# A two-part transformer kernel on one core: a new order in the first stage, weight pieces loaded in halves, and retention's gating and gate row moved

## The chip, the cores and the metric

The kernel runs on one core of one Trainium2 chip as a single launch. The metric is the device time of that launch in microseconds; the time shown is the median of three runs. PE is TensorE, DVE is VectorE, ACT is ScalarE, POOL is GpSimd, SP is the engine that issues the weight loads.

## The reference, cut to what matters

The input is 256 tokens of width 1024 in float32. Two blocks run one after the other, each with two layers. The parts that the change touches are the first mixer of the first block (a gated delta rule over six heads, beside a windowed attention), and in the second block the two mixers (stick-breaking attention and retention).

```
def gated_delta_rule(q, k, v, g, beta):
    ...
    gam = jnp.cumsum(gc, axis=-1)
    decay = jnp.exp(jnp.where(incl, gam[..., :, None] - gam[..., None, :], -jnp.inf))
    kk = jnp.einsum('bhnid,bhnjd->bhnij', kc, kc)
    lower = jnp.eye(c) + jnp.where(strict, bc[..., :, None] * kk * decay, 0.0)
    sol = lax.linalg.triangular_solve(lower, rhs, left_side=True, lower=True, unit_diagonal=True)
...
def even_mixer(x, ...):
    q_a, k_a, v_a, z_a, b_a, a_a, q_b, k_b, v_b = jnp.split(x @ w_in, EVEN_SPLITS, axis=-1)
    qkv = silu(causal_depthwise_conv(concatenate([q_a, k_a, v_a]), conv_w))
    q_a, k_a = l2_normalize(q_a) * GDN_DK ** -0.5, l2_normalize(k_a)
    o_a = gated_delta_rule(q_a, k_a, v_a, g, beta)
    o_a = rms_norm(o_a, norm_w) * silu(z_a)
    o_b = dilated_attention(q_b, k_b, v_b, rel_bias)
    return concatenate([o_a, o_b]) @ w_out
...
def retention(h, positions, w_in, gn_g, w_out):
    q, k, v, g = jnp.split(h @ w_in, [D_MODEL, 2 * D_MODEL, 4 * D_MODEL], axis=-1)
    ...  # per head and chunk of 128: (q k^T * decay mask) v, plus the carried state
    o = ((o - mu) * rsqrt(var + LN_EPS)).reshape(B, S, 2 * D_MODEL) * gn_g
    return (silu(g) * o) @ w_out
...
def second_block(x, c, ...):
    for i in range(DEPTH):
        shift, scale, gate = adaln_params(c, ada_w[i, 0], ada_b[i, 0])
        y = stick_breaking_attention(h, ...) if i == 0 else retention(h, ...)
        x = layer_norm_2(ALPHA * x + (1.0 + gate) * y, ...)
        ...
        y = grouped_moe(h, ...)          # 16 experts
        x = layer_norm_2(ALPHA * x + (1.0 + gate) * y, ...)
```

## The kernel before, in words

Each engine has its own program, written out by hand in stages: `even`, `ffn(0)`, `odd`, `ffn(1)`, `sb_stage`, `moe(0)`, `ret`, `moe(1)`. Nothing is scheduled by a compiler; each engine runs its list in order and waits on counters of the others (`t`, `v`, `a`, `g` are the counters of PE, DVE, ACT and POOL; `t.did(name)` notes a count, `v.wait_ge(*t(name))` waits for it). Where several independent chains run at once, `weave(units, steps, width, fill)` makes the order: round by round one step of each live unit, and after each round one piece of other work, written `(None, k)`. All engines walk the same list.

**First stage, `even`.** Projections are tiles of 128 output channels by 256 tokens; `conv(n)` is one of 24 of them (8 matmuls on PE; for n under 18 a scaled copy on ACT and three fused multiply-adds on DVE; convs 18 to 23 are the gate z, only copied). `L2` weaves the normalization of six pairs of q and k tiles (ACT squares, PE sums over the partitions with a matrix of ones, ACT takes Ln and Exp, DVE multiplies) with convs 12 to 17. `GDN` weaves four units u (a half of the tokens by three heads) of 17 steps with convs 18 to 23 and 13 pieces `ada` of a later modulation, whose weights share the ring of slots. Step 0 of a unit: DVE copies two columns into 128x384 operands (`a`, `b`), PE makes `gdB` and `gdb` from them (three matmuls each), DVE adds the mask into `DT`, ACT takes four exponentials (`gdDT`), and DVE multiplies `LT = DT * gdb`. Step 1 makes `gkk` and `gqk`. After GDN an RMS norm runs over six head tiles of 256 columns, each: square (ACT), sums (PE), Ln, Exp (ACT), two multiplications (DVE). Then `down` multiplies all eight 128-row tiles of the result with `w_out` (pieces `woe`), 32 matmuls of 512 columns; tiles 6 and 7 come from the windowed attention.

**Narrow stages, `sb_stage` and `ret`.** Their weights (`ws`, `wso`, `wr`, `wrv`, `wro`, 2 MB a piece, 24 pieces) come in turn into two slots of the ring. A piece is loaded by SP in one transfer, when the last use of the piece that had the slot before is counted. Each piece is cut into four chunks: ACT rounds a chunk to `ringhi` (`high_half`, four buffers, so chunk i waits for PE to be done with chunk i-4), DVE writes the rest to `ringlo` (`low_half`), and PE multiplies the parts. In `ret`, PE makes 4 + 20 projection tiles (`pr`; the first 16 are q and k, rotated through PE and three DVE operations each; the last eight and then eight more in `GATES` are the gate g), row products of `wrv` (`vr`, 0 to 3, made mean-free on DVE by `centered`), then the gate row of the modulation (`gate_row(2, Q.gk)`: DVE spreads a column to 128x1024, PE turns it with 8 matmuls, DVE copies the result), and then `RETU`: eight heads u of three steps (0: scores `rs`, DVE multiplies by the decay mask into `rp`; 1: values `ro`, ACT squares and copies; 2: sums `rv`, ACT Ln and Exp, DVE scales), three at a time, with the ten pieces `GATES` after the rounds. For u under 4, step 2 on DVE also gates: scale, multiply by the gate, round to `ghi`, subtract to `glo`, for two tiles f = 2u, 2u+1. The other eight tiles are gated inside the last product `down_split` (16 chunks of `wro`, f = 0 to 15, 12 matmuls of 512 columns a chunk).

**MoE stages.** Their expert weights use all eight slots; SP issues each load when its slot is free, in the order of `all_loads`, and stands still at the first load that is not free yet.

Of the kernel before, what the change touches and what calls it, by code (L numbers as in the profile page):

```python
# [175 lines left out]
L2 = weave(6, 2, 3, 6)  # L176
GDN = weave(4, 17, 4, 6 + ADA)
# [7 lines left out]
RETU = weave(8, 3, 3, len(GATES))  # L185

# [21 lines left out]
def all_loads():  # L208
# [15 lines left out]
    out += two[:2] + [("wro", j) for j in range(3)] + two[2:4] + [("wro", 3)] + two[4:]  # L224
# [12 lines left out]
def all_slots():  # L237


    out, used, last, turn, seen, narrow = {}, {}, {}, 0, [0, 0], 0  # L240
    for name in LOADS:
        if name[0] in NARROW:
            i, turn = narrow % 2, 0
            narrow += 1
            last[2] = name
        elif name[0] in ("mg", "mu", "md"):
# [12 lines left out]
PLACE = all_slots()  # L259
def consts():  # L260
# [66 lines left out]
def emit(nc, ctx, ins, out):  # L327
# [57 lines left out]
    s_ring = [sem(f"ring{i}_landed") for i in range(WIDE)]  # L385
    s_row, s_dec = sem("rows_landed"), sem("decay_landed")
# [43 lines left out]
    def chunk(n, i):  # L430

        src, kind, c = CHUNKS[n][i]
        lo = PLACE[src][0] * 4096
        hi = ringhi[:, i % 4, :]
        k = 4 if kind == "D" else 8
        whole, low = (ap[:, lo:lo + 4096].rearrange("p (k n) -> p k n", k=k) for ap in (ring, ringlo))
        if kind == "T":
            at = (slice(None), slice(None), slice(c * 128, c * 128 + 128))
        else:
            at = (slice(None), slice(2 * c, 2 * c + 2) if kind == "R" else slice(c, c + 1), slice(None))  # L440
        return whole[at], hi.rearrange("p (k n) -> p k n", k={"T": 8, "R": 2, "D": 1}[kind]), low[at]
# [31 lines left out]
    with ExitStack() as st:  # L473
# [18 lines left out]
        E.tmp3 = [E.u[i][k] for i in range(2) for k in ("a", "DT", "LT")]  # L492
# [67 lines left out]
    with ExitStack() as st:  # L560
# [11 lines left out]
        Q.gk = m.ap[:, m.top:m.top + 1024]  # L572
# [37 lines left out]
    def tensor():  # L610
# [32 lines left out]
        def first_tiles(n, src, tag, xT=xT):  # L643


            view = slot(src, 8)

            def half(c, h):
                tk = slice(h * 128, h * 128 + 128)
                for k in range(8):  # L650
                    r = mm(banks[c][:, tk], view[:, k, c * 128:c * 128 + 128], xT[:, k, tk], k == 0, k == 7)
                return r

            turn_x(n, 0)
            t.wait_ge(*arrived(src))
# [81 lines left out]
        def down_split(n, tag, i0, high, low, ready):  # L737
# [5 lines left out]
            for f, h in order:  # L743
                _, hi, lo = chunk(n, i0 + f)
# [93 lines left out]
        def even():  # L838
# [76 lines left out]
            for n in range(6):  # L915
# [398 lines left out]
        def ret():  # L1314
# [7 lines left out]
            gate_row(2, Q.gk, v)  # L1322
            i = 28
            for u, k in RETU:
# [24 lines left out]
                else:  # L1349
# [5 lines left out]
                       lambda f: v("gsplit", f))  # L1355
# [14 lines left out]
    def vector():  # L1370
# [119 lines left out]
        def even():  # L1490
# [63 lines left out]
            v.wait_ge(*a("l2", 5))  # L1554
            for u, k in GDN:
                if u is None:
                    ada_piece(0, k - 6)
# [3 lines left out]
            for n in range(6):  # L1561
                v.wait_ge(*a("rms", n))
                o = E.oT[:, n, :]
                tt(o, o, E.tmp3[n][:, 0:256], ALU.mult).then_inc(s_dve, v.did())
                stt(o, o, C("gnw"), E.QT[:, 18 + n, :], ALU.mult, ALU.mult).then_inc(s_dve, v.did("rms", n))
# [45 lines left out]

        def gdn(u, k):
# [7 lines left out]
            if k == 0:  # L1620
                copy(v3(m["a"]), col3(36, n0)).then_inc(s_dve, v.did())
                copy(v3(m["b"]), col3(24, n0)).then_inc(s_dve, v.did("gd_ab", u))
                tt(v3(m["DT"]), v3(src("gdB", u)), k3("cmt"), ALU.add).then_inc(s_dve, v.did("gdDT", u))
                v.wait_ge(*a("gdDT", u))
                tt(m["LT"], m["DT"], src("gdb", u), ALU.mult).then_inc(s_dve, v.did("free", "gdb", u))
# [435 lines left out]
        def ret():  # L2061
# [52 lines left out]
            gate_row(2, Q.gk)  # L2114

            def gated(u, d, o):
                g_ = Q.gT[:, 2 * u + d, :]
                stt(g_, o, C("rgn", 2 * u + d, 2 * u + d + 1), g_, ALU.mult, ALU.mult).then_inc(s_dve, v.did("rout", u))
                v.note("gated", 2 * u + d)

            def gated_low(u, d):
                f = 2 * u + d
# [5 lines left out]
            for u, k in RETU:  # L2128
                if u is None:
# [4 lines left out]
                    if kind == "vr":  # L2134
                        centered(j)
                    continue
# [9 lines left out]
                elif k == 2:  # L2146
                    v.wait_ge(*a("rv", u))
                    for d in range(2):
                        od = o[:, d * 256:d * 256 + 256]
                        if u < 4:  # L2150
                            tt(od, od, w[:, 0:256], ALU.mult).then_inc(s_dve, v.did())
                            v.wait_ge(*a("gT", 2 * u + d))
                            gated(u, d, od)
                            copy(Q.ghi[:, u + 8 * d, :], Q.gT[:, 2 * u + d, :]).then_inc(s_dve, v.did())
                            gated_low(u, d)
                        else:
                            tt(Q.qk[:, u + 8 * d, :], od, w[:, 0:256], ALU.mult).then_inc(s_dve, v.did("unit", u))
            for f in range(16):
                low_half(6, i + f + 3)
                if f < 8:  # L2160
                    u, d = 4 + f // 2, f % 2
                    v.wait_ge(*a("gT", 8 if u < 6 else 12))
                    gated(u, d, Q.qk[:, u + 8 * d, :])
                if 0 < f < 9:
                    v.wait_ge(*a("ghi", 7 + f))
                    gated_low(4 + (f - 1) // 2, (f - 1) % 2)
# [14 lines left out]
    def scalar():  # L2181
# [41 lines left out]
        def high_half(n, i):  # L2223
            if i < len(CHUNKS[n]):
                part, hi, _ = chunk(n, i)
                a.wait_ge(*arrived(CHUNKS[n][i][0]))
# [25 lines left out]
        def even():  # L2252
# [82 lines left out]
            a.wait_ge(*v("go", 3))  # L2335
            for n in range(6):
                act(E.tmp3[n][:, 0:256], E.oT[:, n, :], ACT.Square).then_inc(s_act, a.did("rms_sq", n))
                rms(("rms", n), E.tmp3[n][:, 0:256], ps("rms", n)[:, 0:256], 1.0 / 128, 1e-6)
# [283 lines left out]
        def ret():  # L2622
# [28 lines left out]
            tables("natural_log_exp_and_others")  # L2651
            i = 28
            for u, k in RETU:
                if u is None:
# [4 lines left out]
                    if kind == "g":  # L2659
                        a.wait_ge(*t("pr", 16 + j))  # L2660
                        copy(Q.gT[:, j, :], ps("pr", 16 + j)[:, 0:256]).then_inc(s_act, a.did("free", "pr", 16 + j))
                    continue
                o, w = Q.otmp[u % 3], Q.tmpr[u % 3]
                if k == 1:
                    a.wait_ge(*t("ro", u))
                    if u >= 3:
                        a.wait_ge(*v("rout" if u < 7 else "unit", u - 3))
# [5 lines left out]
            for f in range(16):  # L2673
# [4 lines left out]
                if 0 < f < 9:  # L2678
                    u, d = 4 + (f - 1) // 2, (f - 1) % 2
                    a.wait_ge(*v("gated", 2 * u + d))  # L2680
                    copy(Q.ghi[:, u + 8 * d, :], Q.gT[:, 2 * u + d, :]).then_inc(s_act, a.did("ghi", 2 * u + d))
# [157 lines left out]
    def sync():  # L2839
        def load(name, src):  # L2840
            i, _, old = PLACE[name]
            if i < SLOTS:
# [168 lines left out]
```

## Time and profile before

| | us |
|---|---|
| median of three runs | 2008.42 (2007.47 to 2011.91) |
| profiled execution, its own time | 2009.65 |
| its span in the trace | 2007.9 |
| PE busy (matmuls) | 1768.4 (88%) |
| DVE busy | 918.8 (46%) |
| ACT busy | 653.3 (33%) |

PE is busy for most of the span, so time can only be won where PE stands still or runs at a lower granted clock. The profile's chain of waits covers less than one per cent of the span here, so the stages were read from the timelines of the engines: a row there is a run of alike instructions with its start, its length, the count of records and, in brackets, how long the engine had been idle before it and what ended that. A float32 matmul leaves two records. The span splits into `even` (0 to 391 us), the FFN and odd stages (to 1023), `sb_stage` (to 1180), `moe(0)` (to 1453), `ret` (to 1711) and `moe(1)`.

### The profile page before, as it was taken

Reading aid. Unit: us, or ns where it says so; the run is one execution under the profiler, and the core shown is the slowest. Engines: PE = TensorE matmul, PEld = TensorE weight load, DVE = VectorE, ACT = ScalarE, POOL = GpSimd, SP = SyncE. Lnnn points to the kernel's source line nnn. Section 1 sums busy time; section 2 is a strip of 40 time slices with the busy share of each in tenths; the row PEclk is TensorE's granted clock in tenths of the full one; section 3 lists DMA queues with packets and bytes.
Section 4 is the critical chain, followed back from the end, with each engine's and each line's share of the span. In section 5 each row is a group of like instructions: output and inputs, shape, how many; then the busy total and the mean of one; then the engine's idle time right before and its main releaser. Section 6 shows DMA issues by size and latency. Waiting matters only on the chain. (4 is left out here: it accounts for less than half of the span.)

```text
span 2007.9 us, 25424 instructions
## 1 busy us (share of the span) xinstructions
PE 1768.4 (88%) x10310; PEld 1308.8 (65%) x10310; DVE 918.8 (46%) x1763; ACT 653.3 (33%) x1095; POOL 231.4 (12%) x217
## 2 busy tenths in 40 slices
PE   7988899799999979899989779989879899799884
PEld 6676786399878645699779654434478787544442
DVE  1264543366642444566545463222167665522224
ACT  1024222356631224466433731111134345311110
POOL 0000000053302021333102202000000200020000
PEclk9899899899999989899989889999989999799998
DMA  7322158344452277444426256999653445599992
GB/s 284 129 80 88 43 199 341 119 147 174 157 206 105 100 298 286 175 169 169 147 110 255 118 210 280 428 426 427 260 192 132 173 179 210 202 424 427 427 427 103
DMA packets 33562, 443.00 MB, mean 221 GB/s; under 512 B 3869, under 2 KB 4129, under 8 KB 6945
## 3 DMA queue, kind: packets, MB, share of 16 engines
q1 hardware_dynamic: 29520, 426.78, 53.1%
q0 software_dynamic: 2480, 8.92, 1.3%
q10 hardware_dynamic: 1440, 5.61, 0.7%
q8 instruction: 84, 1.38, 0.3%
q14 instruction: 38, 0.30, 0.0%
HBM read 440.25 MB, written 1.05 MB: 220 GB/s over the span
## 5 line engine op out<-in xcount | busy, mean ns | idle before, releaser
L82 PE MATMUL ps<-ringx,arena 128*64 128x512 f32 x1056 | 277.5, 600 | 23.6 <-DMA ringx<-in_mu 8.6
L88 ACT ACTIVATE arena<-ps 128x384 f32<-128x384 f32 (+5 forms) x233 | 101.6, 436 | 564.8 <-PE ps L82 344.0
L82 PE MATMUL ps<-xsplit_f,wsplit_f 128*128 128x256 f32 x2112 | 259.7, 286 | 17.1 <-DVE xsplit_f L91 12.3
L82 PEld LDWEIGHTS ps<-xsplit_f,wsplit_f 128*128 128x128 f32 x2112 | 257.4, 194 | 19.7 <-DVE xsplit_f L91 13.0
L82 PE MATMUL ps<-ring,arena 128*64 128x512 f32 (+1 forms) x704 | 227.2, 598 | 8.2 <-DMA ring<-in_mg 4.5
L82 PEld LDWEIGHTS ps<-ringx,arena 128*64 128x64 f32 x1056 | 91.3, 138 | 193.1 <-issue 177.2
L82 PE MATMUL ps<-xTs,ring 128*128 128x256 f32 (+1 forms) x960 | 193.1, 362 | 5.5 <-ACT xTs L88 5.5
L91 DVE TENSOR_TENSOR wsplit_f<-ring,wsplit_f 128x1024 fp32r<-128x1024 f32 x132 | 164.1, 1251 | 52.3 <-ACT wsplit_f L88 52.3
L82 PEld LDWEIGHTS ps<-xTs,ring 128*128 128x128 f32 x960 | 167.1, 199 | 28.0 <-issue 10.2
L99 DVE SCALAR_TENSOR_TENSOR arena<-ps,cp_sb,arena 128x255 f32<-128x255 f32 (+2 forms) x230 | 110.8, 482 | 130.6 <-ACT arena L88 114.1
L88 ACT ACTIVATE wsplit_f<-ring 128x1024 fp32r<-128x1024 f32 x132 | 137.5, 1051 | 51.5 <-PE ps L82 51.1
L91 DVE TENSOR_TENSOR ringlo<-ring,ringhi 128x1024 fp32r<-128x1024 f32 x88 | 114.7, 1322 | 82.9 <-ACT ringhi L88 82.7
L82 PE MATMUL ps<-arena 128*128 128x128 f32 (+5 forms) x1128 | 141.5, 303 | 5.8 <-DVE arena L91 5.5
L91 POOL TENSOR_TENSOR small<-small,half 128x1 f32<-128x1 f32 x16 | 8.9, 555 | 1144.5 <-DVE small L95 1144.5
L82 PEld LDWEIGHTS ps<-arena 128*128 128x128 f32 (+2 forms) x1128 | 127.5, 191 | 20.0 <-DVE arena L91 6.5
L82 PEld LDWEIGHTS ps<-ring,arena 128*64 128x64 f32 (+1 forms) x704 | 79.4, 148 | 92.4 <-issue 86.9
L91 DVE TENSOR_TENSOR arena<-arena,ps 128x384 f32<-128x384 f32 (+2 forms) x74 | 42.9, 579 | 199.8 <-PE ps L82 183.4
L82 PE MATMUL ps<-wsplit_f,gsplit 128*128 128x512 f32 x528 | 122.5, 394 | 5.5 <-DVE wsplit_f L91 5.5
L88 ACT ACTIVATE ringhi<-ring 128x1024 fp32r<-128x1024 f32 x88 | 90.7, 1051 | 94.4 <-PE ps L82 40.0
L91 POOL TENSOR_TENSOR arena<-arena 128x256 f32<-128x256 f32 (+1 forms) x58 | 89.3, 1540 | 256.1 <-DVE arena L99 132.3
L82 PEld LDWEIGHTS ps<-wsplit_f,gsplit 128*128 128x128 f32 x528 | 99.9, 190 | 27.6 <-DVE wsplit_f L91 6.7
L91 POOL TENSOR_TENSOR xs<-xs,lnp 128x1024 f32<-128x1024 f32 x28 | 70.0, 2509 | 254.0 <-DVE ringlo L91 98.8
(175 smaller groups left out, 2454.7 us busy)
## 6 DMA issues: line engine op xcount, KB each, us to landing
ring<-in_ada SPq DMA_DIRECT2D x24, 2048.0 KB, 8.3
ring<-in_wu SPq DMA_DIRECT2D x22, 2048.0 KB, 8.0
ringx<-in_mg SPq DMA_DIRECT2D x22, 2048.0 KB, 22.1
ringx<-in_mu SPq DMA_DIRECT2D x22, 2048.0 KB, 24.9
ringx<-in_md SPq DMA_DIRECT2D x22, 2048.0 KB, 25.7
ring<-in_md SPq DMA_DIRECT2D x12, 2048.0 KB, 27.4
ring<-in_mg SPq DMA_DIRECT2D x12, 2048.0 KB, 22.1
ring<-in_mu SPq DMA_DIRECT2D x12, 2048.0 KB, 25.9
```

The lines of the kernel that those rows point to most:

```text
L82: return self.e.matmul(o, l, r, start=start, stop=stop, skip_group_check=True)
L88: return self.e.activation(o, i, f, **k)
L91: return self.e.tensor_tensor(o, a, b, op)
L99: return self.e.scalar_tensor_tensor(out=o, in0=a, scalar=s, in1=b, op0=op0, op1=op1)
```

## The change

Six edits, all of order and placement; the arithmetic is the same.

1. `L2` puts one conv ahead of the woven list. `GDN` puts step 0 of all four units together, then convs 18 and 19, then the rest. The two column copies of units 1 to 3 move into L2 (`gdn_columns`), those of unit 0 to its end.
2. The RMS norm runs over three pairs of 512 columns, and PE begins the output product with tiles 6 and 7 around it (`block`).
3. Narrow pieces are loaded in two halves of 1 MB with a counter each; a half waits only for the two chunks that had its place. The host lays the column pieces out chunk by chunk, so that a chunk is contiguous.
4. All four `wro` pieces stand ahead of the second pair of `mu` loads in the order of loads.
5. Retention's gate row moves from ahead of RETU into `down_split`, before f = 10 (on DVE behind f = 9); its operand moves to `xTs`.
6. Retention's gating of tiles 0 to 7 leaves step 2; `GATED` spreads it behind the pieces 4 to 7 of GATES, with the rounding on ACT and the subtraction a piece later.

```
-L2 = weave(6, 2, 3, 6)
-GDN = weave(4, 17, 4, 6 + ADA)
+L2 = [(None, 0)] + [(u, k if u is not None else k + 1) for u, k in weave(6, 2, 3, 5)]
+
+GDN = [(u, 0) for u in range(4)] + [(None, 0), (None, 1)] \
+    + [(u, k + 1 if u is not None else k + 2) for u, k in weave(4, 16, 4, 4 + ADA)]
...
+GATED = {4: (0, 1), 5: (2, 3, 4, 5), 6: (6,), 7: (7,)}
...
-    out += two[:2] + [("wro", j) for j in range(3)] + two[2:4] + [("wro", 3)] + two[4:]
+    out += two[:2] + [("wro", j) for j in range(4)] + two[2:]
...
+                if h == 0 and f in among:
+                    among[f]()
...
+            t.wait_ge(*arrived(("woe", 1)))
+            t.wait_ge(*a("swo"))
+            for h in range(2):
+                block(6, h)
+            for n in range(3):
                 t.wait_ge(*a("rms_sq", n))
-                rms_sums(("rms", n), E.tmp3[n][:, 0:256])
+                rms_sums(("rms", n), E.sq[n])
             t.note("early", 0)
-            t.wait_ge(*v("rms", 5))
-            t.wait_ge(*a("swo"))
-            down([("woe", 0), ("woe", 1)], ("dn", 0), E.oT)
+            for h in range(2):
+                block(7, h)
+            t.wait_ge(*arrived(("woe", 0)))
+            t.wait_ge(*v("rms", 0))
+            for k, h in ((0, 0), (0, 1), (1, 0), (1, 1)):
+                block(k, h)
+            for h in range(2):
+                for k in range(2, 6):
+                    t.wait_ge(*v("rms", k // 2))
+                    r = block(k, h)
...
-            gate_row(2, Q.gk, v)
...
-                       lambda f: v("gsplit", f))
+                       lambda f: v("gsplit", f), {10: lambda: gate_row(2, Q.gk, v)})
...
+                    if 2 <= k < 5:
+                        gdn_columns(k - 1)
...
+                    for f in GATED.get(k - 1, ()):
+                        gated_low(f)
+                    for f in GATED.get(k, ()):
+                        gated(f)
...
+            if name[0] in NARROW:
+                for h in range(2):
+                    if old in FIRST:
+                        n, first = FIRST[old]
+                        s.wait_ge(*t("part", n, first + 2 * h + 1))
+                    else:
+                        s.wait_ge(*(t("used", old) if ("used", old) in t.at else v("used", old)))
+                    lo = 2048 * h
+                    s.dma_start(ring[:, i * 4096 + lo:i * 4096 + lo + 2048], src[:, lo:lo + 2048]).then_inc(s_half[2 * i + h], 16)
+                return
```

On DVE, between L2 and the first steps of GDN: `arena<-small` are the column copies, `arena<-ps,kc_sb` the mask additions, `arena<-arena,ps` the products with `gdb` (and behind them with `gkk` and `gqk`).

```order
 L102 COPY arena<-small 128x384 x2
-L91 TENSOR_TENSOR arena<-ps,kc_sb 128x384
-L91 TENSOR_TENSOR arena<-arena,ps 128x384
-L102 COPY arena<-small 128x384 x2
-L91 TENSOR_TENSOR arena<-ps,kc_sb 128x384
-L91 TENSOR_TENSOR arena<-arena,ps 128x384
-L102 COPY arena<-small 128x384 x2
-L91 TENSOR_TENSOR arena<-ps,kc_sb 128x384
-L91 TENSOR_TENSOR arena<-arena,ps 128x384 x3
+L91 TENSOR_TENSOR arena<-ps,kc_sb 128x384 x4
+L91 TENSOR_TENSOR arena<-arena,ps 128x384 x6
```

The copies no longer stand between one unit's product and the next unit's addition; in the new list four additions and then the products follow each other.

On PE, where the first stage ends: `ring,gate` and `small,tmpn` are the last ada pieces, `arena,ones` the RMS sums, `ring,arena` the output product.

```order
 L82 MATMUL ps<-ring,gate 32x512 x8
-L82 MATMUL ps<-small,tmpn 128x1 x4
-L82 MATMUL ps<-ring,gate 32x512 x8
 L82 MATMUL ps<-small,tmpn 128x1 x8
-L82 MATMUL ps<-arena,ones 128x256 x6
-L82 MATMUL ps<-ring,arena 128x512 x32
+L82 MATMUL ps<-ring,arena 128x512 x4
+L82 MATMUL ps<-arena,ones 128x512 x3
+L82 MATMUL ps<-ring,arena 128x512 x28
```

Four of the 32 matmuls of the product stand ahead of the sums, and the six sums have become three of twice the width.

On DVE in RETU, behind the last `centered` (its last operation is the first row): `gated<-arena,gated` is the subtraction, `arena<-arena,cp_sb` the gating product, `arena<-ps,kc_sb` the mask products `rp` of heads 6 and 7.

```order
 L91 TENSOR_TENSOR arena<-ps,small 128x512
+L91 TENSOR_TENSOR gated<-arena,gated 128x256 x2
+L99 SCALAR_TENSOR_TENSOR arena<-arena,cp_sb 128x256 x4
 L91 TENSOR_TENSOR arena<-ps,kc_sb 128x256
 L91 TENSOR_TENSOR arena<-ps,kc_sb 128x128
 L91 TENSOR_TENSOR arena<-ps,kc_sb 128x256
 L91 TENSOR_TENSOR arena<-ps,kc_sb 128x128
```

Six operations now stand between `centered` and `rp` of head 6.

## Rows read from the trace of the kernel before

**Rows 1.** windows: us, busy of each engine, granted clock (PEclk), DMA share, GB/s
```profile
196.00:225.00 29.00, 16.70 (x67) 14.57 (x66) 10.31 (x19) 7.25 (x17) 0.00 (x0) 0.65 0.00 1
366.00:368.00 2.00, 2.00 (x5) 0.78 (x4) 1.30 (x2) 0.00 (x0) 0.00 (x0) 0.87 0.00 0
1751.00:1950.00 199.00, 184.82 (x914) 80.82 (x912) 50.51 (x176) 27.71 (x55) 10.56 (x6) 0.99 1.00 422
```

**Rows 2.** timeline of PE, first stage: start, us, what, [idle before, releaser]
```profile
173.68 2.84 PE L82 MATMUL ps<-arena,ones 128*128 128x512 f32 x6 [3.66 <-ACT arena L88]
...
199.75 2.90 PE L82 MATMUL ps<-kc_sb,arena 128*128 128x128 f32 x12 [3.38 <-DVE arena L102]
...
217.06 2.93 PE L82 MATMUL ps<-kc_sb,arena 128*128 128x128 f32 x12 [2.96 <-DVE arena L102]
219.78 5.29 PE L82 MATMUL ps<-xTs,ring 128*128 128x256 f32 x16
224.91 5.52 PE L82 MATMUL ps<-arena 128*128 128x128 f32 x48
```

**Rows 3.** timeline of DVE, first stage
```profile
203.87 0.55 DVE L91 TENSOR_TENSOR arena<-arena,ps 128x384 f32<-128x384 f32 x1 [1.91 <-ACT arena L88]
```

**Rows 4.** timeline of ACT, first stage
```profile
173.00 1.95 ACT L88 ACTIVATE arena<-arena 128x512 f32<-128x512 f32 x3
```

**Rows 5.** timeline of PE, end of the first stage
```profile
345.13 0.68 PE L82 MATMUL ps<-arena,ones 128*128 128x256 f32 x2
347.27 1.22 PE L82 MATMUL ps<-arena,ones 128*128 128x256 f32 x2 [1.46 <-ACT arena L88]
...
361.20 30.36 PE L82 MATMUL ps<-ring,arena 128*128 128x512 f32 x64 [1.99 <-DVE arena L99]
```

**Rows 6.** timeline of the DMA-issuing queue, first stage
```profile
335.00 5.95 SPq L114 DMA_DIRECT2D ring<-in_woe  x2
```

**Rows 7.** timeline of PE, retention stage
```profile
1535.07 0.36 PE L82 MATMUL ps<-xth,ringhi 128*128 128x256 f32 x1 [0.58 <-DVE ringlo L91]
...
1583.98 3.78 PE L82 MATMUL ps<-kc_sb,arena 128*128 128x128 f32 x16 [7.52 <-DVE arena L102]
1587.56 2.59 PE L82 MATMUL ps<-arena 128*128 128x256 f32 x12
...
1622.46 5.86 PE L82 MATMUL ps<-arena 128*128 128x256 f32 x24 [4.32 <-DVE arena L91]
...
1644.57 1.47 PE L82 MATMUL ps<-arena 128*128 128x256 f32 x8
...
1648.75 2.85 PE L82 MATMUL ps<-arena 128*128 128x256 f32 x16
...
1697.70 0.80 PE L82 MATMUL ps<-ringhi,gated 128*128 128x512 f32 x1 [2.14 <-DVE ringlo L91]
```

**Rows 8.** timeline of DVE, retention stage
```profile
1576.26 3.50 DVE L91 TENSOR_TENSOR ringlo<-ring,ringhi 128x1024 fp32r<-128x1024 f32 x3 [2.69 <-ACT ringhi L88]
...
1583.23 0.69 DVE L102 COPY arena<-mods 128x1024 f32<-128x1024 f32 x1
...
1609.71 0.42 DVE L91 TENSOR_TENSOR arena<-arena 128x256 f32<-128x256 f32 x1 [1.25 <-ACT arena L88]
1610.17 0.48 DVE L99 SCALAR_TENSOR_TENSOR arena<-arena,cp_sb 128x256 f32<-128x256 f32 x1
...
1621.66 2.46 DVE L91 TENSOR_TENSOR arena<-ps,kc_sb 128x256 f32<-128x256 f32 x6
```

**Rows 9.** DMA issues: KB each, median us to landing
```profile
ring<-in_wr SPq DMA_DIRECT2D x8, 2048.0 KB, 7.5
...
ring<-in_wdl SPq DMA_DIRECT2D x2, 1024.0 KB, 4.7
```

**Rows 10.** timeline of ACT, retention stage
```profile
1494.10 1.06 ACT L88 ACTIVATE ringhi<-ring 128x1024 fp32r<-128x1024 f32 x1 [2.07 <-DMA ring<-in_wr]
```

**Rows 11.** timeline of the DMA-issuing queue, retention stage
```profile
1684.45 0.33 SPq L114 DMA_DIRECT2D ring<-in_wro  x1
```

More of the change, by code:

```diff
@@ L243, in all_slots @@
             i, turn = narrow % 2, 0
+            out[name] = (i, narrow // 2 + 1, last.get(i))
             narrow += 1
-            last[2] = name
-        elif name[0] in ("mg", "mu", "md"):
+            last[i] = last[2] = name
+            continue
+        if name[0] in ("mg", "mu", "md"):
             k = seen[name[1]] % WIDE
@@ L259 @@
 PLACE = all_slots()
+FIRST = {src: (n, i) for n, ch in CHUNKS.items() for i, (src, _, c) in enumerate(ch) if c == 0}
 def consts():
@@ L385, in emit @@
     s_ring = [sem(f"ring{i}_landed") for i in range(WIDE)]
+    s_half = [sem(f"half{i}_landed") for i in range(4)]
     s_row, s_dec = sem("rows_landed"), sem("decay_landed")
@@ L432, in chunk, with half_arrived @@
         src, kind, c = CHUNKS[n][i]
[L433 to L441, printed above, removed]
+        lo = PLACE[src][0] * 4096 + 1024 * c
+        parts = ring[:, lo:lo + 1024], ringhi[:, i % 4, :], ringlo[:, lo:lo + 1024]
+        return [ap.rearrange("p (k n) -> p k n", k={"T": 8, "R": 2, "D": 1}[kind]) for ap in parts]
+    def half_arrived(name, h):
+        n, count, _ = PLACE[name]
+        return s_half[2 * n + h], 16 * count
     def arrived(name):
@@ L735, in rows_split, with down_split @@
             t.note("used", src)
-        def down_split(n, tag, i0, high, low, ready):
+        def down_split(n, tag, i0, high, low, ready, among={}):
             banks = [bank(tag, i) for i in range(4)]
@@ L1554, in even @@
             v.wait_ge(*a("l2", 5))
+            gdn_columns(0)
             for u, k in GDN:
                 if u is None:
+                    if k == 0:
+                        for i in range(4):
+                            v.wait_ge(*a("gdDT", i))
+                            v.wait_ge(*t("gdb", i))
+                            tt(E.u[i]["LT"], E.u[i]["DT"], ps("gdb", i)[:, 0:384], ALU.mult).then_inc(s_dve, v.did("free", "gdb", i))
                     ada_piece(0, k - 6)
@@ L2148, in ret @@
                     for d in range(2):
[L2149 to L2157, printed above, removed]
+                        tt(Q.qk[:, u + 8 * d, :], o[:, d * 256:d * 256 + 256], w[:, 0:256], ALU.mult).then_inc(s_dve, v.did("unit", u))
             for f in range(16):
                 low_half(6, i + f + 3)
+                if 0 < f < 9:
+                    gated_low(7 + f)
                 if f < 8:
[L2161 to L2166, printed above, removed]
+                    gated(8 + f)
+                if f == 9:
+                    gate_row(2, Q.gk)
             norm(6, lambda i: ps(("dn", 6), i), True)
@@ L2334, in even @@
                     tables("natural_log_exp_and_others")
[L2335 to L2338, printed above, removed]
+            for n in range(3):
+                a.wait_ge(*v("go", 3 if n else 2))
+                act(E.sq[n].rearrange("p (t n) -> p t n", t=2), E.oT[:, 2 * n:2 * n + 2, :], ACT.Square).then_inc(s_act, a.did("rms_sq", n))
+            for n in range(3):
+                rms(("rms", n), E.sq[n], ps("rms", n), 1.0 / 128, 1e-6)
             a.note("early", 0)
@@ L2651, in ret, with gated_high @@
             tables("natural_log_exp_and_others")
+            def gated_high(f):
+                a.wait_ge(*v("gated", f))
+                copy(Q.ghi[:, f // 2 + 8 * (f % 2), :], Q.gT[:, f, :]).then_inc(s_act, a.did("ghi", f))
             i = 28
@@ L2666, in ret @@
                     if u >= 3:
-                        a.wait_ge(*v("rout" if u < 7 else "unit", u - 3))
+                        a.wait_ge(*v("unit", u - 3))
                     act(w, ps("ro", u), ACT.Square).then_inc(s_act, a.did("rsq", u))
@@ L2677, in ret @@
                     act(Q.gT[:, j:j + 4, :], Q.gT[:, j:j + 4, :], ACT.Silu).then_inc(s_act, a.did("gT", j))
[L2678 to L2681, printed above, removed]
+                if f < 8:
+                    gated_high(8 + f)
             tables("natural_log_exp_and_others")
```

70 lines of the change are left out of this document (46 added, 24 removed).

## The prediction

> **What bounds the kernel now.** I read the page first: PE is busy for 88% of the span, so only its idle time and its time at the lower clock can be saved. Next I took PE's timeline of the first stage and of retention, and kept the rows with a bracket. In the first stage the reader is to see two clusters. At the head of the gated delta rule PE waits four times for DVE, and works at half clock between the waits: [rows 2] has the first wait (3.38 us) and the last (2.96), the two between are 3.00 and 2.96 long; the granted clock of the stretch is 0.65 in [rows 1]. At the stage's end six sums of 256 columns come 2.68 us apart, 1.46 of it waiting ([rows 5]), until the output product starts at 361.20. In retention [rows 7] shows a wait of 7.52 us for DVE before the gate row, one of 4.32 before the value products of heads 3 to 5, one of 2.14 in the last product, and five of 0.58 in the rotated tiles. In `sb_stage` I found no wait of PE for a weight: its tiles run without a gap, so the halves can win nothing there. `moe(1)` moves 422 GB/s at a DMA share of 1.00 ([rows 1]); it is bound by its loads.
>
> **1. One conv ahead in L2.** PE sits idle for 3.66 us before the first sums, because ACT squares only from 173.00 ([rows 2, 4]). Now conv 13 runs there. A conv takes 3.5 us (half of the 7.07 us of two, in the same timeline), but ACT first does the scaled copy of conv 12 (0.5 us), so the sums start at about 174.2, and PE waits 0.7 us. Saved: 2.9.
>
> **2. The head of GDN.** Unit 0's columns are still copied last, behind conv 17, so the first wait stays (3.4). The other three waits go, 3.00 + 2.96 + 2.96 = 8.9, since the columns are there. In the new list PE makes all four groups and two convs while ACT and DVE work through the exponentials: DVE waits for ACT once a unit ([rows 3]), about 1.8 us each, 7.3 in all, and four groups and two convs are at least 12.5 us of PE. That cover hides the chain; without it, 7 us of wait would come back. The clock: twelve records of a group take 1.38 us at full clock (5.52/48 x 12), but 2.90, 2.56, 2.93, 2.93 here, 11.3 in all, and conv 18 takes 5.29 instead of 3.6 ([rows 2]). After an idle stretch of 3.4 us the clock was low from 199.75 and high again about 4 us later; in the new list PE goes on working, so I count 4 us at half clock and the rest at full: 7.6 for the four groups. Saved: 8.9 + 3.7 + 1.7 = 14.3.
>
> **3. The RMS norm and the output product.** Before: 16.07 us from 345.13 to 361.20, then 30.36. The product ran at half clock until about 367 ([rows 1]: 0.87 in the slice from 366), 5.8 us, which cost 2.7 (the bound at the other end is nothing, if the clock falls again). New: the product and three sums. Six records of 512 columns took 2.84 ([rows 2]). ACT and DVE need about 4 us from the first sums to the first normalized pair (Ln, Exp and two products of 512 columns, 0.7 each, and the sums' 0.9); the other two sums and tile 7 cover 5 us. 30.36 - 2.7 + 2.84 = 30.5 against 46.43. One new wait: PE begins with `woe` 1. Its load was issued at 340.6 ([rows 6], the second of two, 5.95 - 0.33 after the first), when ada piece 10 was done, and took about 7 us; in the new list PE has 7.4 us of work between that point and tile 6. I count 0.5. Saved: 15.4.
>
> **4. Retention.** (a) ACT waits 2.07 us for `wr` 2 at its first chunk ([rows 10]). A 2 MB piece lands 7.5 us after issue, 1 MB after 4.7 ([rows 9]); the loop of ACT and DVE that paces the rotated tiles starts 2 us sooner, and takes it from the five waits of 0.58 ([rows 7]). Saved: 2.0. (b) Without the gate row, the scores of head 0 follow at 1576.46 (1583.98 - 7.52) instead of 1587.56: 11.1. DVE has split the next chunks by 1579.8 ([rows 8]) and is done with `centered` at 1583.2, then needs 2.5 for the masks and 1.2 for the fourth chunk of `wrv` 2: 1586.9, and PE comes to that chunk at 1587. Nothing new is late. (c) The 4.32 us: DVE ran 24 gating operations between 1609.71 and 1620.4, then a split, then the masks at 1621.66 ([rows 8]). Six scalings of 0.42 to 0.46 remain, so the masks come 8 us sooner. Saved: 4.3, and 1.8 of low clock (5.86 us for 24 records against 4.1). (d) `wro` 3 was issued at 1684.45 ([rows 11]), when its slot was free; its first half now goes at about 1678.6, two chunks of 2.8 us sooner. The wait of 2.14 goes, with 1.4 of low clock behind it. Saved: 3.5. (e) The gate row costs PE 1.9 in the product (its 3.78 were at half clock), nothing on DVE's side that PE waits for.
>
> (f) What it adds on the path: behind `centered` of `vr` 3, DVE now does two subtractions (0.43) and four gating products (0.48, [rows 8]) before the masks of heads 6 and 7. In the kernel before, those masks were ready just as PE came to the values at 1648.75, 4.2 us after the scores began at 1644.57 ([rows 7]). So PE waits 2.9 there. ACT, behind the same gating, is 3 us later with the squares of head 6, which I estimate costs 0.5 more before the sums, and 0.8 of clock. Cost: 4.2. Bounds: nothing if DVE has run ahead, 8 if the clock stays low through the last four tiles.
>
> **The sum.** First stage 2.9 + 14.3 + 15.4 = 32.6. Retention 2.0 + 11.1 + 6.1 + 3.5 - 1.9 - 4.2 = 16.6. In all 49.2, from the profiled execution's 2009.65: 1960.4. The median before is 1.2 below that execution, so the forecast is 1959.
>
> **A page against the trace.** Rows of 2 MB and 1 MB say 7.5 and 4.7 us ([rows 9]): two halves in a row, each waited for alone, are 9.4 us, under the 11.5 that PE needs for a piece (96 matmuls that start 0.12 apart in its timeline). The Trainium skill, DMA: Bandwidth & Descriptors, Rules for kernel authors, speaks against cutting: gather many small transfers into one large one. [...]
>
> **Rivals.** *A, as summed:* 66%, 1951 to 1967.
> *B, the spread gating is worse than (f):* ACT's rounding waits for DVE and DVE's subtraction for ACT, in every piece from the fourth on. If each of pieces 4 to 8 loses 2 us, retention wins 7 instead of 17: 1969. For it: ACT and DVE each wait for the other in [rows 7, 8] already. Against: DVE is idle 5 us before its split in that round. 12%.
> *C, the clock stays low through the head of GDN:* the first 3.4 us wait is still there. Groups and both convs at half clock cost 11.3 + 10.6 instead of 7.6 + 7.1: 7 us more, 1966. Against: in the product of [rows 5], work without a gap brought it back within 6 us. 8%. The Trainium skill, TensorE: Matmul & The Clock Gate, Part 1, says that the throttled state is the default and that activity lifts it; by this rule the trace agrees with A.
> *D, `moe(1)` gives retention's part back,* being bound by its loads: 1976. Against: its refills wait for the use of slots by its own products, so they move with it; and the first eight pieces have landed before it starts. 5%.
> *E, the halves do not come sooner* (SP issues in order, and a half behind another wait stands still): (a) and (d) are lost, 1964.5. 6%.
> *F, slower:* each half takes as long as a whole piece, 7.5, so 15.0 a piece against 11.5 of PE, on some 20 of the 24 pieces: 70 us lost, 49 won, about 2029. It decides from 7.0 us a half. Against: the 1 MB row. 3%.
>
> **The numbers.** No change could be told within 0.2% (4 us). All but F, and remnants where several terms fail together, are far faster: faster 0.96, same 0.01, slower 0.03. The range takes in A, B's and C's sizes, E, and the unknown wait (f) from 0 to 8 with the clock's return: 1949 to 1973. That leaves out D, F and the worst of B, under 2 in 10.
>
> **What would show it.** In PE's timeline: no wait between the four groups, and a product of about 28 us at full clock around three sums (else step 3); RETU's scores right behind `vr` 1, and a new wait of about 3 us before the values of heads 6 and 7 (else f); no wait in the last product. The granted clock over the head of GDN should be high from about 4 us on (else C). ACT's first chunk of `wr` 2 should wait less than 0.5 us (else E). The prediction is wrong above all if the wait at tile 6 is long, or if GDN's later rounds, which now start earlier, wait for ACT.

## The result, and the profile after

The changed kernel takes 1978.45 us (median of 4 runs, 1974.8 to 1979.17), the kernel before, measured beside it, 2008.45: a ratio of 0.9844, 95% interval 0.9827 to 0.9861. It is 30 us faster. The forecast was 1959, with 1949 to 1973 as its range: the direction is right, and 19 us of the gain are missing. The profiled execution is one of 1974.8 us, with a span of 1973.1 against 2007.9 before, so the traces account for 34.8. It is the fastest of the four, 3.6 us under the median.

The first stage and the end of `sb_stage`, in PE's timeline (start, us, what, idle before and releaser):

```profile
174.11 2.84 PE L82 MATMUL ps<-arena,ones 128*128 128x512 f32 x6 [0.71 <-ACT arena L88]
...
196.72 8.54 PE L82 MATMUL ps<-kc_sb,arena 128*128 128x128 f32 x48 [3.38 <-DVE arena L102]
205.10 7.07 PE L82 MATMUL ps<-xTs,ring 128*128 128x256 f32 x32
...
329.07 3.67 PE L82 MATMUL ps<-ring,arena 128*128 128x512 f32 x8
332.58 2.74 PE L82 MATMUL ps<-arena,ones 128*128 128x512 f32 x6
335.15 24.20 PE L82 MATMUL ps<-ring,arena 128*128 128x512 f32 x56
...
1123.55 0.47 PE L82 MATMUL ps<-ringhi,xth 128*128 128x512 f32 x1 [2.93 <-DVE oTlo L91]
...
1434.90 1.94 PE L85 MATMUL ps<-kc_sb,xs 128*128 128x128 f32 x8 [13.43 <-DVE tmpn L91]
```

The first six rows answer to [rows 2, 5]. The four groups are one row without a wait (8.54 us), both convs run at full clock (7.07, granted clock 1.00), and the three sums stand inside the output product. The last two rows are new waits, in stages that the forecast left alone: PE waits 2.93 us before `sb_stage`'s product, where the kernel before waited for nothing, and 13.43 before it turns `x` for retention, where the kernel before has this row:

```profile
1462.38 1.97 PE L85 MATMUL ps<-kc_sb,xs 128*128 128x128 f32 x8 [8.81 <-DVE xs L96]
```

Retention, PE again; these rows answer to [rows 7]:

```profile
1604.28 2.89 PE L82 MATMUL ps<-arena 128*128 128x256 f32 x16 [2.87 <-DVE arena L91]
...
1638.03 0.51 PE L82 MATMUL ps<-ringhi,gated 128*128 128x512 f32 x1 [0.55 <-DVE ringlo L91]
...
1641.67 0.50 PE L82 MATMUL ps<-ringhi,gated 128*128 128x512 f32 x1 [0.59 <-DVE ringlo L91]
...
1645.31 0.50 PE L82 MATMUL ps<-ringhi,gated 128*128 128x512 f32 x1 [0.59 <-DVE ringlo L91]
...
1654.90 3.78 PE L82 MATMUL ps<-kc_sb,xTs 128*128 128x128 f32 x16 [6.53 <-DVE xTs L102]
```

The waits of 7.52, 4.32 and 2.14 us are gone. In their place stand the 2.87 that the forecast had, three waits exactly 3.64 us apart, and 6.53 before the gate row. The windows say what followed (us, busy of each engine, granted clock, DMA share, GB/s):

```profile
1636.00:1654.90 18.90, 10.64 (x43) 7.41 (x41) 12.02 (x16) 8.07 (x11) 0.00 (x0) 0.96 0.82 327
1654.90:1660.00 5.10, 5.10 (x20) 4.81 (x21) 1.97 (x3) 0.00 (x0) 0.00 (x0) 0.50 0.00 0
```

PE is busy for 10.6 of the 18.9 us before the gate row. Behind it the clock is at the lower of its two levels (0.50, that is 1.2 GHz) for 5.1 us, and the row takes 3.78 us where it takes 2.05 at full clock (`lag_back`, below): the wait is paid twice.

**Where the two traces part.** Starts of the same work, after minus before: at `ffn(0)` -32.2 us; at `sb_stage` -37.2 (`odd()` waits 2.24 us for `wov` in place of 5.51, and feed-forward 1 has less of the low clock: 1.00 against 0.94 in one stretch of 30 us); at `moe(0)` -32.8 and at its end -32.1; at the start of retention -27.5; at its last product -44.0; at `moe(1)` -34.4. So 4.4 us were lost at the end of `sb_stage`, 4.6 between `moe(0)` and retention, and 9.6 within the last product, which takes 58.5 us where it took 48.9.

What paces the last product stands in the timelines of DVE and ACT there:

```profile
1636.75 1.23 DVE L91 TENSOR_TENSOR ringlo<-ring,ringhi 128x1024 fp32r<-128x1024 f32 x1 [1.44 <-ACT ringhi L88]
1638.01 0.43 DVE L91 TENSOR_TENSOR gated<-arena,gated 128x256 fp32r<-128x256 f32 x1
1638.47 0.48 DVE L99 SCALAR_TENSOR_TENSOR arena<-arena,cp_sb 128x256 f32<-128x256 f32 x1
1640.39 1.23 DVE L91 TENSOR_TENSOR ringlo<-ring,ringhi 128x1024 fp32r<-128x1024 f32 x1 [1.43 <-ACT ringhi L88]
...
1652.90 1.22 DVE L91 TENSOR_TENSOR ringlo<-ring,ringhi 128x1024 fp32r<-128x1024 f32 x1
1654.15 0.69 DVE L102 COPY xTs<-mods 128x1024 f32<-128x1024 f32 x1
```
```profile
1638.99 0.42 ACT L88 ACTIVATE gated<-arena 128x256 fp32r<-128x256 f32 x1 [2.27 <-DVE arena L99]
1639.32 1.04 ACT L88 ACTIVATE ringhi<-ring 128x1024 fp32r<-128x1024 f32 x1
```

Read them as one loop. DVE gates a tile (to 1638.95); ACT, which stood still for 2.27 us, rounds that tile and then the next chunk (to 1640.36); DVE, which stood still for 1.43, subtracts the chunk, then the tile, and only then gates the next. Neither engine is full, and a chunk takes 3.64 us. PE needs 2.8. The last DVE row is the copy for the gate row: it stands behind the split of the thirteenth chunk, so behind the whole loop, and PE behind it.

### The profile page after: what moved, and what is told of

Its sections match the earlier page's. It is cut to its first block and busy times, and to the rows that moved or that the text cites. A ratio compares the mean times of both kernels' runs of the same rounds, so it can differ in the third digit from the quotient of the medians.

```text
span 1973.1 us, 25429 instructions
## 1 busy us (share of the span) xinstructions
PE 1757.2 (89%) x10304; PEld 1302.5 (66%) x10304; DVE 916.1 (46%) x1749; ACT 654.4 (33%) x1094; POOL 231.8 (12%) x217
```

## The experiments

Times are medians of five executions (four of `first_only`), ratios are against nine executions of the kernel before that were measured beside them, and gains are against the changed kernel's 1978.45. There were three such sets, in which the kernel before had 2007.88 (`first_only` to `lag_back`), 2009.22 (the two with banks, `all_fixes`, `all_later`) and 2008.06 (the others). By the ratios every difference given here comes out within 2 us of that by medians.

**The ladder: how much each part brings.** `first_only` holds the edits of `L2`, `GDN` and the RMS norm alone.

> The kernel before with the edits of the first stage alone (one conv ahead in L2, the new order at the head of GDN, the joined RMS norm and the output product that starts with tile 6); loads, retention and the gate row are those of before. Theory 1, the parts are separate: the first stage gives its 32.2 us and odd() 2.7, the loss of 4.4 us at the end of sb_stage belongs to the halves and is absent, so about 2008.4 - 34.9 = 1973.5. Theory 2, sb_stage's end and the way into retention lose because everything ahead of them is earlier: 4.4 and 4.6 are lost here too, 1978 to 1982. Retention lasts as long as before (its last product 48.9 us in PE's timeline) in both.

1985.16 us, ratio 0.9889 (0.9874 to 0.9905): 23 us, not 35. The first stage's trace is that of the changed kernel, and both new waits are here:

```profile
1127.92 0.47 PE L82 MATMUL ps<-ringhi,xth 128*128 128x512 f32 x1 [2.92 <-DVE oTlo L91]
...
1437.51 1.94 PE L85 MATMUL ps<-kc_sb,xs 128*128 128x128 f32 x8 [11.69 <-DVE tmpn L91]
```

So the loss has nothing to do with the halves, and theory 1 fell: an edit of the first stage makes PE wait over 700 us later. `first_halves` adds the half pieces and `wro` 3's new place:

> The one before plus the half pieces and the new place of wro 3 in the list of loads; gate row and gating as before. Theory 1, the halves bring 2.4 us in the rotated tiles and 3.5 in the last product, and cost 4.4 at the end of sb_stage: 1973.5 - 5.9 + 4.4 = 1972. Theory 2, sb_stage's loss has nothing to do with the halves: 1.5 to 6 us less than the kernel with the first stage alone, and the wait of 2.93 us for oTlo stands in both kernels or in neither.

1976.97 us, 0.9842 (0.9826 to 0.9857): 8.2 us less. Four waits of 0.58 in the rotated tiles became two, the one before the gate row fell from 8.64 to 4.46 us, and the 2.24 in the last product went. `row_in_product` adds the gate row's new place:

```
 in DVE's loop of the last product (gating as in the kernel before)
+                if f == 9:
+                    gate_row(2, Q.gk)
 in PE's
+ down_split(..., {10: lambda: gate_row(2, Q.gk, v)})
```

> The one before plus the gate row inside the last product (DVE copies and evacuates it behind the split of chunk 12), gating still as in the kernel before, where ACT rounds a gated tile one piece behind DVE. Theory 1, the chain between ACT and DVE (a piece of gating that waits in both directions within one chunk, 0.42 + 1.05 + 1.23 + 0.43 + 0.48 = 3.6 us and PE needs 2.8) made the product long in the changed kernel: here there is no such chain, so 11.1 us are won before RETU and the row costs 2 to 4: 7 to 9 us less than the kernel with halves. Theory 2, the row's place itself is at fault, since its copy stands behind a split that DVE can only do when PE has left a slot: PE waits 5 us or more before the row here too, and 3 to 5 us are won at most.

1971.9 us, 0.9812 (0.9798 to 0.9827): 5.1 us less. PE waits 0.40 us before the row, though the row stands where it does in the changed kernel:

```profile
1655.29 2.05 PE L82 MATMUL ps<-kc_sb,xTs 128*128 128x128 f32 x16 [0.40 <-DVE xTs L102]
```

By the wait, theory 1 holds: the place alone does no harm. The gain is below its 7 to 9, because with the halves the row ahead of `RETU` cost less than theory 1 took from the kernel before: 4.46 us of wait and 3.38 of matmuls, against 0.40 and 2.05 in the product, is 5.4. The part that is left to the changed kernel, the spread gating, then costs 6.5 us where it should have saved. It is a bigger edit than its name says: it also moves the rounding of tiles 0 to 7 from DVE to ACT, and it changes the order in the last product.

**The loop between ACT and DVE.** `lag_back` is the changed kernel with this alone:

```
 DVE, last product
                 low_half(6, i + f + 3)
-                if 0 < f < 9:
-                    gated_low(7 + f)
                 if f < 8:
                     gated(8 + f)
+                if 0 < f < 9:
+                    gated_low(7 + f)
 ACT, last product
-                if f < 8:
-                    gated_high(8 + f)
+                if 0 < f < 9:
+                    gated_high(7 + f)
```

> The changed kernel, with ACT again rounding a gated tile of the last product one piece behind DVE (and DVE gating a tile before it subtracts the one before), as the kernel before has it. Theory 1, the chain: DVE's period falls from 3.64 to 2.2 us a piece, the waits of 0.55 to 0.59 before chunks go and most of the 6.53 us before the gate row with its low clock: the last product takes 49 to 51 us instead of 58.5, about 1970. Theory 2, the row's place: the three short waits go, the one before the row stays over 4 us: 1975 to 1977. Theory 3, the loads of wro land late by halves: nothing changes, 1978.

1968.26 us, 0.9801 (0.9787 to 0.9814): 10.2 us less, and the last product takes 47.3 us. DVE's period is 2.3 us where nothing else holds it (2.34 between the two splits below), and ACT rounds a tile that was gated a piece ago:

```profile
1637.45 1.22 DVE L91 TENSOR_TENSOR ringlo<-ring,ringhi 128x1024 fp32r<-128x1024 f32 x1
1638.70 0.48 DVE L99 SCALAR_TENSOR_TENSOR arena<-arena,cp_sb 128x256 f32<-128x256 f32 x1
1639.29 0.43 DVE L91 TENSOR_TENSOR gated<-arena,gated 128x256 fp32r<-128x256 f32 x1
1639.79 1.22 DVE L91 TENSOR_TENSOR ringlo<-ring,ringhi 128x1024 fp32r<-128x1024 f32 x1
```
```profile
1652.95 2.05 PE L82 MATMUL ps<-kc_sb,xTs 128*128 128x128 f32 x16 [0.40 <-DVE xTs L102]
```

No wait is left before a chunk, the row costs 2.05 at full clock, and the loads are innocent. `copy_early` keeps the loop and takes only the copy away from behind it (DVE copies gate 2's columns at `f == 1`, once the last gate tile is done, and evacuates the gate at `f == 12`):

> The changed kernel (1978.4) with its chain between ACT and DVE as it is, but gate 2's columns copied by DVE early in the last product (behind the first gated tile but one), and the gate evacuated behind the last split. The wait of 6.53 us before the gate row stands in the trace at the copy. Theory 1, chain plus place (the copy comes late because twelve splits at 3.64 us stand ahead of it): the wait before the row goes with its low clock (1.7), the short waits of 0.55 to 0.59 stay: 6 to 8 us less, 1971. Theory 2, the chain alone (PE is short of splits anyhow, and the wait moves to the next chunk): 0 to 2 us less.

1970.01 us, 0.9804 (0.9782 to 0.9826): 8.4 us less. PE keeps its three short waits and comes to the row without one:

```profile
1651.40 0.50 PE L82 MATMUL ps<-ringhi,gated 128*128 128x512 f32 x1 [0.57 <-DVE ringlo L91]
...
1654.29 1.95 PE L82 MATMUL ps<-kc_sb,xTs 128*128 128x128 f32 x16
```

The loop and the place do their harm together. Either repair alone brings nearly all, since what costs is the copy being late, and it is late only when both hold. The loop by itself costs little: its three short waits are 1.7 us, and the two medians lie 1.75 apart, less than the spread of `copy_early` (1964.5 to 1972.9).

**The banks.** A tile of PSUM is given the next of eight banks in turn, and PE waits until the last user of that bank has been read (`Banks.take`, `bank`). The joined norm takes three sums where six were, so from then on every tile that goes by this turn stands three places off. (`sbz` and `sbo` have rings of their own, banks 0 to 3 and 4 to 7, so the tiles behind them meet other users.) Counted through the code: `sb_stage`'s product stood on banks 0 to 3, last used by `("sbz", 12)` to `("sbz", 15)`; now it stands on 5, 6, 7 and 0, and the last users of 5, 6 and 7 are `("sbo", 13)` to `("sbo", 15)`, which DVE has still to read. And `("xT", 6, 0, 0)` now stands on bank 3 behind `("acc", 5, 3)`, the last quarter of the other half's sum, where it stood on bank 6 behind `("y", 5, 11, 0)`. (`acc` and `y` are tiles of the last experts of `moe(0)`.) Both kernels get one line at the end of `even()` on PE:

```
+            ps.turn[R8] += 3
             t.note("pre", 0)
```

> The kernel with the first stage alone (1985.2), plus one line: three places are skipped in the rotation of PSUM banks at the end of the first stage. That stage now asks for three banks fewer (three sums of squares instead of six), and every later tile sits three banks further on. Theory 1, banks: the product of sb_stage then stands on banks that were free, as before, and PE's wait of 2.92 us for oTlo goes (with 1.5 of low clock behind it); the turning of x into retention no longer stands behind the last tile of the other half's norm, 3.0 us; in all 7.4, so about 1978, and retention starts 32 to 34 us sooner than in the kernel before. Theory 2, the earlier start as such (where the instructions and the clock's phase fall): both waits stay, 1985.

> The changed kernel (1978.4) with the same line, three places skipped in the rotation of PSUM banks. Theory 1, banks: 4.4 at the end of sb_stage and 3.0 at the start of retention come back, 1971. Theory 2: 1978. In both the last product stays at 57 to 59 us.

`first_banks`: 1973.14 us, 0.9825 (0.9802 to 0.9848), 12.0 below `first_only`. `banks_back`: 1968.77 us, 0.9797 (0.9779 to 0.9815), 9.7 below the changed kernel. Each wins more than the 7.4 expected. In neither does PE wait for `oTlo`, and the turn goes as soon as half 0 is normalized. The row of `first_banks`, then that of `banks_back`:

```profile
1429.05 1.97 PE L85 MATMUL ps<-kc_sb,xs 128*128 128x128 f32 x8 [8.70 <-DVE xs L96]
```
```profile
1427.92 1.97 PE L85 MATMUL ps<-kc_sb,xs 128*128 128x128 f32 x8 [8.97 <-DVE xs L96]
...
1638.10 0.50 PE L82 MATMUL ps<-ringhi,gated 128*128 128x512 f32 x1 [0.59 <-DVE ringlo L91]
...
1647.69 3.78 PE L82 MATMUL ps<-kc_sb,xTs 128*128 128x128 f32 x16 [6.54 <-DVE xTs L102]
```

The last two rows show the loop and the late copy untouched, so the two causes are separate. From PE's first wait for POOL in `sb_stage` to the turn of `x` behind its product the changed kernel takes 74.3 us (1074.09 to 1148.42), `banks_back` 69.8, the kernel before 69.9.

**All repairs together.** `all_fixes` has the order of `lag_back`, the copy of `copy_early`, and the three banks.

> The changed kernel with three edits: the rounding by ACT one piece behind again (lag_back, 1968.3), gate 2's columns copied by DVE early in the last product and its evacuation behind the last split, and the three banks skipped. If the causes are separate, lag_back's 10.2 us, 0.4 for the copy and 7.4 for the banks add up: 1978.4 - 18 = 1960.5, which is the time forecast for the change itself. If the two waits for banks only hid other waits: 1964 to 1968.

1957.37 us, 0.9743 (0.9726 to 0.976): 21 us less than the changed kernel, and 52 less than the kernel before. It is also 1.6 under the time forecast for the change itself. The remaining edits were tried on it. `row_ahead` puts the gate row back ahead of `RETU`:

> The kernel with all three repairs (1957.4), but with the gate row ahead of RETU as in the kernel before. The forecast gave that place 11.1 us (a wait of 7.52 and 3.78 of PE at the lower clock) against 1.9 in the product. If that holds, 9 us more, 1966.5. With half pieces ahead of it DVE comes sooner: the kernel with the first stage and halves shows a wait of 4.46 us and not 7.52 there, so by the second theory it is 4.5 + 3.8 - 2.0 = 6 us more, 1963.5.

1966.12 us, 0.9787 (0.9767 to 0.9808): 8.8 more by medians, 7.6 by retention's length in the traces (238.6 against 231.0). The wait there is the second theory's, and the row runs at the lower clock:

```profile
1552.76 3.44 PE L82 MATMUL ps<-kc_sb,arena 128*128 128x128 f32 x16 [4.50 <-DVE arena L102]
```

That is 7.9 us, less 2.0 for the row in the product, so 6 as that theory has it. The rest of the 7.6 is low clock elsewhere: the values of heads 6 and 7 take 4.55 us in this trace and 2.88 in that of `all_fixes`. The five times run from 1961.95 to 1971.45, so they cannot tell 6 from 9.

`whole_pieces` loads the narrow pieces in one transfer each:

> The kernel with all three repairs (1957.4), with each piece of ws, wso, wr, wrv and wro loaded by one transfer of 2 MB, issued when all four chunks of the old piece are used, and waited for as a whole; layout and order of the loads as they are. The forecast gave the halves 2.0 in the rotated tiles and most of 3.5 in the last product: 3 to 5 us more, 1961 to 1963. If they are worth what the two kernels with the first stage showed apart (8.2 us with the new place of wro 3): 1965. If the halves are hidden by now: 1957.

1961.1 us, 0.977 (0.9753 to 0.9788): 3.7 more, within 3 to 5. Its trace has the waits of 0.58 five times again (0.50 to 0.59), and retention takes 232.6 us against 231.0; some 2 of the 3.7 are not found there. No wait returns to the last product, so what took away the 2.24 in `first_halves` need not have been the halves. The likely cause is `wro` 3's place in the list, though it was not tried alone. That place does not bring the issue forward: in the kernel before as in `whole_pieces` it goes when its slot is free, at 1684.45 and 1638.47. But in the kernel before two `mu` loads had been issued 11 us ahead of it, and ACT begins its first chunk 10.9 us after the issue; in `whole_pieces` they stand behind it, and ACT begins after 7.5.

The last two ask whether the 2.87 us before the values of heads 6 and 7 can be had.

```
-GATED = {4: (0, 1), 5: (2, 3, 4, 5), 6: (6,), 7: (7,)}
+GATED = {6: (0, 1, 2, 3), 7: (4, 5, 6), 8: (7,)}          # all_later
+GATED = {4: (0, 1), 6: (2, 3, 4), 7: (5, 6), 8: (7,)}     # gating_mid
```

> The one before, with the gating of tiles 0 to 7 not ahead of the masks of heads 6 and 7 but behind them (tiles 0 to 3 with piece 6, 4 to 6 with piece 7, 7 with piece 8). If DVE's four gating products and two subtractions there make the wait of 2.87 us before the values of heads 6 and 7, it goes, with 0.8 of low clock: 3 to 4 us less than the one before. If that wait is moved to the sums of heads 6 and 7 or into the first chunks of the last product instead: the same time, or 1 to 3 us more.

> The kernel with all three repairs (1957.4), with tiles 0 and 1 gated with piece 4 as in the changed kernel, 2 to 4 with piece 6, 5 and 6 with piece 7, 7 with piece 8. Putting all of them behind the masks of heads 6 and 7 took PE's 2.87 us away there and gave 1.27 and 1.50 back in the first chunks of the last product. If it is a matter of where the work lies, this middle way keeps a wait of 0.9 to 1.4 for the masks and under 1 in the product: 1 to 2 us less. If DVE is simply full from the masks to the fourth split, the sum of these waits stays at 2.8 and the time the same.

1956.95 us (0.9738, 0.9721 to 0.9755) and 1956.35 us (0.9744, 0.9726 to 0.9763); neither can be told from `all_fixes`. `all_later` has no wait for the masks, and gets these in the last product:

```profile
1614.22 0.50 PE L82 MATMUL ps<-ringhi,gated 128*128 128x512 f32 x1 [1.27 <-DVE ringlo L91]
```
```profile
1618.78 0.51 PE L82 MATMUL ps<-ringhi,gated 128*128 128x512 f32 x1 [1.50 <-DVE ringlo L91]
```

2.87 removed, 2.77 returned: the wait moved. `gating_mid` has 0.79 for the masks and 1.04 in the product, 1.0 less in all, which is below what these runs resolve.

## Why the prediction was right, and where it was wrong

- **First stage (forecast 32.6).** Right, step by step: 32.2. The sums started at 174.11 after 0.71 us (174.2 and 0.7 were forecast), the first wait of 3.38 stayed and the other three went, the groups took 8.54 instead of 7.6 (the clock was low for the first 6.2 us, not 4), the whole end 30.2 instead of 30.5, and tile 6 did not wait.
- **Retention up to its last product (2.0 + 11.1 + 6.1 - 4.2 = 15.0).** Right: 16.5. In the kernel before the first of the five waits called 0.58 is one of 0.32; two are left, and 1.5 us of these waits were won. The new wait (f) measured 2.87 us against 2.9. The 11.1 of (b) are in the traces of before and after; the part of it that the row's place earns is smaller once the halves stand ahead of it, since the wait there is then 4.5 us and not 7.52.
- **The step that failed: (e), "nothing on DVE's side that PE waits for",** and with it the waitless product of (d). The product should have become 1.6 us shorter and became 9.6 longer: 11.2 of the 14.4 us that the traces miss. The row was priced as 16 matmuls. Neither the copy that stands ahead of it on DVE nor what stands ahead of that copy was followed. The gains of (d) were there: `lag_back` has the 47.3 us that the forecast gives the product (48.9 - 3.5 + 1.9), though the 3.5 was put down to half pieces, and may belong to the list's order. With the loop the copy came at 1654.15, with the order of before it cost 0.40.
- **The loop was in rival B,** "ACT's rounding waits for DVE and DVE's subtraction for ACT", but for the pieces of `RETU`, where it costs nothing. It was not looked for in the last product, where the diff changes the lag of both engines at once: ACT's `0 < f < 9` became `f < 8`, and DVE's two steps changed places. Each edit reads as tidying; together they close the ring. Rival B's size came out all the same: retention as a whole won 6.9 us, and B says 7. That is chance, since what was lost was lost elsewhere.
- **Left out of the sum: the banks.** The forecast costed the three sums by their matmuls, and never counted what taking three banks fewer does to the rest of the program. In the traces that is 4.5 us in `sb_stage` and 2.9 in front of retention; undone, it gave 9.7 and 12.0 by medians. The 5.0 us that `odd()` and feed-forward 1 gained were not in the sum either, and hid part of it.
- The sum of the repairs (21.1) is near that of its parts (10.2 and 9.7). With both causes out of the way the kernel runs at 1957, where the forecast put the change. In that trace retention wins 18.1 us where the forecast has 16.6, and `sb_stage`'s first wait for POOL comes 35.0 sooner where it has 32.6, so the prices that it did write down were good. That the totals meet so closely is in part luck: 2 to 5 us between the first stage and `sb_stage` were in no sum.
- Rivals C, D, E and F did not come true: the convs ran at full clock, `moe(1)` kept retention's end (-34.4 before it, -34.8 at the end), and the halves came sooner and cost nothing: those of `wr` took 5.4 us to land (median), longer than the 4.7 of the sum and well under the 7.0 at which F begins.

What stays open: by medians `banks_back` and `first_banks` won 2.3 and 4.6 us more than 7.4. The trace of `banks_back` is just 7.4 us shorter than the changed kernel's. Of the 13.8 us between the traces of `first_only` and `first_banks`, retention holds 5.6, above all because the wait before the gate row is 5.56 us and not 8.64; whether that hangs on the banks, no run tells. A part of the rest is in the next section.

## What to carry to other kernels

Where buffers or banks are given out in turn, an edit that changes how many are taken moves every later tile to another one: compare, behind the edit, on whose bank each tile lands, above all a product that starts while its predecessor is being read, and restore the phase by skipping places. Where two engines hand work to each other in one loop, keep a step between giving and taking; if both wait for this step's result, the loop runs at the sum of their times while each looks half idle. And before an operation is put within a stream, ask what stands ahead of its first instruction on every engine that it uses, not only what it costs on the engine that sets the time.

## What was not expected of the hardware

Two stretches differ between executions though nothing was edited in them. Between two of the 3.5 us waits for POOL in `sb_stage`, the changed kernel takes 12.30 us and `first_only` 13.88 (windows of the one, then of the other). It is not the code: `lag_back` and `copy_early`, which are the changed kernel up to the last product of retention, take 13.89 and 13.82.

```profile
1087.40:1099.70 12.30, 8.79 (x56) 7.37 (x56) 6.83 (x14) 8.97 (x18) 3.20 (x8) 0.88 0.00 0
```
```profile
1088.76:1102.64 13.88, 10.37 (x57) 8.66 (x57) 6.84 (x14) 9.02 (x18) 3.22 (x8) 0.75 0.00 0
```

DVE and ACT are busy for the same time; the granted clock of the stretch is 0.88 in the one and 0.75 in the other, and PE takes 1.58 us more for it. After the same wait the clock is at times low for longer. The next stretch shows it again, with 12.54 and 13.76 us.

And the wait between `moe(0)`'s last matmul and the turn of `x` has two values. Where no bank is in the way, eight traces show 8.70 to 9.12 us (five, the 8.81 of the kernel before among them) or 10.40 to 10.47 (three); where one is, 11.67 to 12.00 (three) or 13.30 to 13.65 (three, the changed kernel among them). The bank costs about 2.9 us in either case. The other 1.6 are no edit's either: `copy_early` has 12.00 and the changed kernel 13.43 with the same code up to there. They seem to go to how soon the engines leave the branch of the last experts, though the traces do not show why it varies: DVE's first operation behind it, which the trace puts behind PE's queue, comes 4.4 us after the last matmul's start in the changed kernel and 2.8 in the kernel before.

```profile
1425.52 0.69 DVE L91 TENSOR_TENSOR tmpn<-ps,gate 128x512 f32<-128x512 f32 x1 [6.23 <-PEq L1348]
```

Together these make up to 4.4 us between two executions of one kernel (1.58 and 1.22 in the stretches, 1.6 at the branch). A gain of a few us is therefore not to be read from the spans of two traces alone: look at which stretch it stands in, and take the size from the medians.
